# Where the attention outputs are turned, where the output projection's pieces stand, and a combination in two parts

## The chip, the cores and the metric

The kernel runs on one core of one Trainium2 chip. The metric is the device time of one execution in microseconds, of which the median of several executions is taken. The engines are called PE (TensorE, matrix multiply), ACT (ScalarE), DVE (VectorE), POOL (GpSimd) and SP (SyncE, which only issues transfers here).

## What is computed

Two layers of a transformer trunk on 1024 rows of 1024 columns, in float32. Cut to its core:

```python
for l in range(2):
    h = rmsnorm(x, g_mix[l])
    proj = h @ w_in[l]                       # q, k, v of 12 heads in three groups
    lam = exp(sum(l0 * l1)) - exp(sum(l2 * l3)) + lam_init
    # group A, 4 heads: a = softmax(s1) - lam * softmax(s2); o = rmsnorm(a @ v, g_sub) * (1 - lam_init)
    # group B, 4 heads: sliding window of 128 with sinks
    # group C, 4 heads: forgetting attention (a cumulated log gate is added to the scores)
    x = x + concat([o_a, o_b, o_c]) @ w_out[l]
    h = rmsnorm(x, g_mlp[l])
    x = x + square(relu(h @ w_up[l])) @ w_down[l]
return rmsnorm(x, g_final)
```

## The kernel before

Every large product is made in three passes, since each operand is split into a high and a low part of reduced precision: high by high, low by high, high by low. A **piece** is such a product of one 128x128 block of weights with one chunk of 128 rows of the activations (`accumulate`, L1134): six matmuls of 128x512. ACT makes the high parts (`w_hi`, `wide_hi`, `pt_hi`), DVE or POOL the low parts (`w_lo`, `wide_lo`, `pt_lo`).

In a layer, attention is done by 8 **pairs** of heads in turn (`ORDER`: B, B, C, C, A, A, A, A), each in 8 **steps**, one for each block of 128 query rows, so that step `t` runs from 0 to 63. Pair 6 is steps 48 to 55, and pair 7, the last, is steps 56 to 63. A step of pair A has, in this order of dependence: the scores on PE (`scores`, L1213; two phases when there are more than four key blocks), score plus bias with its row maximum on DVE (`biased_max`, L912), two exponentials on ACT (L638), the combination `a = p1 - lam * p2` on DVE (`combine`, L940), the transposes of the result on PE (`turn_half`, L1266; a **half** is up to four blocks of 128x128 and takes one of the two banks of `ps[2]`), high and low part of the transposed half (L656 on ACT, L963 on DVE), and the products with the values (`values`, L1286 and L1288). The sum of these goes to `o_out` (L972).

Work that does not depend on the step stands between. A step is cut into **slots**, one for each half that is turned in it; PE's order in a slot is scores, pieces, second phase of the scores, turn of the half, and the values of the half of the slot before. `PIECES` says how many pieces a step gets: in pairs 0 to 6 those of the in-projection slabs of the next pair (`FILL`), in pair 7 those of the output projection. An output slab `k` is 128 columns of `w_out`; its pieces go over the eight slabs of `o_out`. `OUT+k` is the number of its weights among the loads. In pair 7 the first three output slabs get six of their eight pieces each (O0, O1 and O2 below), the rest of them comes later from small copies of the weights (`xw_hi`, `xw_lo`). After step 63 comes a tail: output slab 3 in `ps[0]`, the last head's normalisation, and then the output slabs in the order `OFIN`.

Before a slab of `o_out` can be multiplied it is transposed into `wide_hi` and `wide_lo`: eight blocks, in two **mix halves** that use the same `ps[2]` banks, with L651 on ACT and L958 on DVE. `MIX_AT` says in which step each slab's mix halves stand, always at the step's end, in slots of their own. `SCALE_AT` says at which steps the A heads' norms are taken (variances on DVE, a square root on ACT with two table loads, the scaling on POOL). All engines run their programs in order, so that what stands behind a waiting instruction waits too; a turn of half `h` waits for the low part of half `h - 2`.

Of the kernel before, what the change touches and what calls it, by code (L numbers as in the profile page):

```python
# [44 lines left out]
def hybrid_encoder(nc, x, w_in, a_lambda, a_subln, b_sinks, c_fbias, w_out, g_mix, g_mlp,  # L45
# [44 lines left out]
    OFIN = [3, 0, 4, 1, 5, 2, 6, 7]  # L90
# [31 lines left out]
    NPHASE = PHASE0[NT]  # L122

# [3 lines left out]
    PIECES[PAIRS - 1] = [0, 1, 3, 4, 4, 3, 3, 0]  # L127
    MIX_AT = {56: [0, 1], 57: [2, 3], 58: [4, 5], 62: [6]}
    SCALE_AT = {FIRST_A * NQ + 2 * NQ + 3: (0, 2), FIRST_A * NQ + 3 * NQ + 3: (2, 3)}
# [83 lines left out]
    for t in range(NT):  # L213
        now = [s for s in slots if s.step == t]
        wide = phases(t) == 2
        for j in range(2):
            at = (j + 2 if len(now) >= 4 else j) if wide else 0
            now[min(at, len(now) - 1)].exps.append(j)
        now[1 if wide and len(now) >= 4 else 0].second = wide
# [11 lines left out]
    with ExitStack() as ctx:  # L231
# [302 lines left out]
        def _(act):  # L534
# [54 lines left out]
            for l in range(DEPTH):  # L589
# [69 lines left out]
                def finish_o(t):  # L659
# [3 lines left out]
                    if grp == "A":  # L663
                        A.activation(o_junk[:], o_out[:, p, i * P:(i + 1) * P], ACT.Square,
# [27 lines left out]
                if slots[-1].summed is not None:  # L692
                    finish_o(slots[-1].summed)
                finish_o(NT - 1)
                rms_of_heads(3, 4)
                split_load(l, EXTRA + 1)
# [65 lines left out]
        def _(dve):  # L762
# [48 lines left out]
            for l in range(DEPTH):  # L811
# [118 lines left out]
                def combine(t):  # L930
# [9 lines left out]
                    V.scalar_tensor_tensor(out=probs[:, (2 * t) % 4, 0:width], in0=probs[:, (2 * t + 1) % 4, 0:width],  # L940
                                           scalar=lam_ratio[:, c:c + 1], in1=probs[:, (2 * t) % 4, 0:width],
                                           op0=ALU.mult, op1=ALU.add).then_inc(combined, 1)
# [59 lines left out]
                for s in slots:  # L1002
# [3 lines left out]
                    if s.first and t < NT:  # L1006
                        biased_max(t, 0)
                    if s.first and t:
                        if ORDER[(t - 1) // NQ][0] == "A":
                            combine(t - 1)  # L1010
                        else:
                            invert_sums(t - 1)
                    if s.second:
# [18 lines left out]

                sum_values(NT - 1)
# [6 lines left out]
                split_load(l, EXTRA + 1)  # L1040
# [69 lines left out]
        def _(pe):  # L1110
# [40 lines left out]
            for l in range(DEPTH):  # L1151
# [95 lines left out]
                def turn_half(half):  # L1247
# [9 lines left out]
                    elif ORDER[half.step // NQ][0] == "A":  # L1257
                        pe.wait_ge(combined, NQ * AH * l + half.step - NQ * FIRST_A + 1)
# [33 lines left out]

                for s in slots:
# [10 lines left out]
                    dense(s.pieces[early:])  # L1304
                    if s.half:
# [4 lines left out]
                def out_piece(k, slab, p, start, stop):  # L1310
                    j = w_slot(l, OUT + k)
                    return accumulate(p, w_hi[:, j, chunk_of(slab)], w_lo[:, j, chunk_of(slab)], wide_hi[here][:, slab],
                                      wide_lo[here][:, slab], start, stop)

                pe.wait_ge(scores_read, NPHASE * (l + 1))
                pe.wait_ge(w_split, LOADS * l + OUT + 4)
                out_piece(3, 0, 0, True, False)
                out_piece(3, 1, 0, False, False)
                values(slots[-1].half)
                for slab in range(2, NC - 1):  # L1320
                    if slab == LATE:
                        pe.wait_ge(pt_split, NHALF * l + mix_ready[LATE])
                    out_piece(3, slab, 0, False, False)
                for half in MIX_LAST:
                    turn_half(half)
                for f, k in enumerate(OFIN):
                    p = FINAL_OUT_PS[f]
                    if f == 0:
                        pe.wait_ge(pt_split, NHALF * (l + 1))
                        out_piece(k, NC - 1, p, False, True).then_inc(slab_done, 1)  # L1330
                        continue
                    if f == 1:
                        pe.wait_ge(evacuated, EVACS * l + IN + NPARTIAL)
                        pe.wait_ge(w_split, LOADS * l + EXTRA + 1)
# [88 lines left out]
```

## Time and profile before

| | |
|---|---|
| median of 3 executions | 2730.36 us (2727.61 to 2734.29) |
| the profiled execution | 2732.85 us, of it 2730.8 us span |
| PE busy | 2586.2 us, 95% of the span |
| DVE, ACT, POOL busy | 42%, 33%, 8% |
| mean granted clock of PE | 0.98 of full |

The page lists busy times, the chain of work that ended last and groups of instructions; the trace behind it gives each instruction's start, and, for a wait, who ended it.

### The profile page before, as it was taken

What the parts mean: (1) busy time and instruction counts of PE and PEld (TensorE: products, weight loads), DVE (VectorE), ACT (ScalarE), POOL (GpSimd) and SP (SyncE); (2) the same over time, 40 slices, a digit from 0 to 9 for tenths busy, and PEclk for the clock granted to TensorE, in tenths of its full rate; (3) what the DMA queues carried; (4) which work ended last, traced back from release to release, by engine and by line L of the source; (5) the groups of instructions that cost most, each with busy time, mean ns of one, the idle gap of its engine ahead of it and who ended that gap; (6) DMA issues with size and microseconds to landing.
All of it is one profiled execution on the core that took longest, in us unless ns stands there. A gap on an engine that the chain in (4) does not pass through costs nothing.

```text
span 2730.8 us, 33929 instructions
## 1 busy us (share of the span) xinstructions
PE 2586.2 (95%) x12825; PEld 2117.3 (78%) x12825; DVE 1153.6 (42%) x2309; ACT 893.1 (33%) x1572; POOL 216.4 (8%) x101
## 2 busy tenths in 40 slices
PE   7999999879999999999999999987899999999998
PEld 6778777668788888888878777765788888888886
DVE  5555566645322223223336546665542232232233
ACT  4554444433211212112236544444322121120222
POOL 1111111112000000000211111111110000000001
PEclk9999999999999999999999999999999999999999
DMA  5100010211111111111220000002111111111112
GB/s 174 55 24 24 16 32 24 62 39 45 46 47 46 54 46 46 54 46 52 94 86 24 24 24 24 24 24 68 47 39 54 46 46 54 46 46 54 45 47 77
DMA packets 219019, 131.42 MB, mean 48 GB/s; under 512 B 15222, under 2 KB 214432, under 8 KB 218664
## 3 DMA queue, kind: packets, MB, share of 16 engines
q1 hardware_dynamic: 213208, 114.38, 14.5%
q10 hardware_dynamic: 5712, 15.73, 1.5%
q8 instruction: 61, 1.00, 0.2%
q14 instruction: 38, 0.31, 0.0%
HBM read 117.47 MB, written 12.62 MB: 48 GB/s over the span
## 4 chain that ended last, share of the span: by engine, by line
PE 75%; issue 9%; DVE 8%; ACT 6%; DVEq 2%; DMA 0%; SPq 0%; ACTq 0%; POOL 0%; POOLq 0%
PE ps L1134 67%; DVE probs L912 2%; PE ps L1266 2%; PE ps L1286 2%; ACT probs L638 2%; ACT pt_hi L656 2%; PE ps L1213 1%; PE ps L1288 1%; DVEq L919 1%; DVE pt_lo L963 1%; DVE probs L940 1%; DVE neg_max L927 1%; ACT sink_exp L641 1%; DVE part L823 0%; PE ps L1115 0%
## 5 line engine op out<-in xcount | busy, mean ns | idle before, releaser
L1134 PE MATMUL ps<-wide_hi,w_hi 128*128 128x512 f32 x3016 | 960.1, 400 | 41.2 <-DVE v_parts L833 10.6
L1134 PE MATMUL ps<-wide_lo,w_hi 128*128 128x512 f32 x3016 | 939.7, 393 | 0.0
L1134 PE MATMUL ps<-wide_hi,w_lo 128*128 128x512 f32 x3016 | 937.6, 392 | 0.0
L1134 PEld LDWEIGHTS ps<-wide_hi,w_hi 128*128 128x128 f32 x3016 | 553.7, 190 | 176.7 <-issue 54.9
L1134 PEld LDWEIGHTS ps<-wide_hi,w_lo 128*128 128x128 f32 x3016 | 571.8, 190 | 122.6
L1134 PEld LDWEIGHTS ps<-wide_lo,w_hi 128*128 128x128 f32 x3016 | 571.5, 190 | 122.5
L638 ACT ACTIVATE probs<-probs,neg_max,slope 128x256 f32<-128x256 f32 (+7 forms) x256 | 202.4, 791 | 339.1 <-DVE neg_max L927 275.3
L714 ACT ACTIVATE w_hi<-w_raw 128x1024 fp32r<-128x1024 f32 x112 | 117.8, 1052 | 453.0 <-PE ps L1134 443.5
L963 DVE TENSOR_TENSOR pt_lo<-ps,pt_hi 128x512 fp32r<-128x512 f32 (+3 forms) x216 | 126.6, 586 | 262.1 <-ACT pt_hi L656 261.7
L718 ACT ACTIVATE ring<-ring 128x1024 f32<-128x1024 f32 x64 | 67.8, 1060 | 491.0 <-DVE ring L1069 491.0
L1089 DVE TENSOR_TENSOR xt<-ps,xt 128x1024 f32 x48 | 58.8, 1225 | 387.1 <-PE ps L1134 387.1
L1069 DVE SCALAR_TENSOR_TENSOR ring<-ps,inv_rms 128x1024 f32<-128x1024 f32 x64 | 78.4, 1225 | 330.0 <-PE ps L1134 313.2
L1286 PE MATMUL ps<-v_parts,pt_hi 128*128 128x128 f32 (+1 forms) x696 | 187.2, 331 | 27.8 <-DVE pt_lo L963 27.6
L510 POOL TENSOR_TENSOR w_lo<-w_raw,w_hi 128x1024 fp32r<-128x1024 f32 x50 | 121.8, 2436 | 950.6 <-ACT w_hi L546 950.6
L1286 PEld LDWEIGHTS ps<-v_parts,pt_hi 128*128 128x128 f32 x696 | 137.0, 197 | 38.6 <-DVE pt_lo L963 37.0
L1288 PE MATMUL ps<-v_parts,pt_lo 128*128 128x64 f32 (+1 forms) x696 | 160.8, 240 | 0.0
L656 ACT ACTIVATE pt_hi<-ps 128x512 fp32r<-128x512 f32 (+3 forms) x216 | 109.0, 505 | 136.3 <-PE ps L1266 135.8
L1072 DVE TENSOR_TENSOR wide_lo<-ring,wide_hi 128x1024 f32 x64 | 78.4, 1226 | 158.1 <-ACT wide_hi L720 158.1
L1266 PE MATMUL ps<-ident,probs 128*128 128x128 f32 x696 | 117.7, 284 | 28.5 <-DVE probs L940 28.3
L1288 PEld LDWEIGHTS ps<-v_parts,pt_lo 128*128 128x128 f32 x696 | 138.0, 198 | 0.1
L1065 DVE TENSOR_TENSOR w_lo<-w_raw,w_hi 128x1024 fp32r<-128x1024 f32 x112 | 136.4, 1218 | 2.2 <-ACT w_hi L714 2.2
L1266 PEld LDWEIGHTS ps<-ident,probs 128*128 128x128 f32 x696 | 86.6, 145 | 57.6 <-issue 40.4
(139 smaller groups left out, 1836.5 us busy)
## 6 DMA issues: line engine op xcount, KB each, us to landing
w_raw<-in_w_up_dram SPq DMA_DIRECT2D x128, 256.0 KB, 3.0
w_raw<-in_w_down_dram SPq DMA_DIRECT2D x128, 256.0 KB, 3.0
w_raw<-in_w_in_dram SPq DMA_DIRECT2D x92, 256.0 KB, 3.3
x_saved<-xt ACTq DMA_DIRECT2D x16, 512.0 KB, 2.6
w_raw<-in_w_out_dram SPq DMA_DIRECT2D x32, 256.0 KB, 3.3
xt<-x_saved SPq DMA_DIRECT2D x16, 512.0 KB, 3.7
o_out<-cum_saved ACTq DMA_DIRECT2D x2, 2048.0 KB, 8.1
out_dram<-rows SPq DMA_DIRECT2D x4, 1024.0 KB, 5.7
```

What stands on the lines that cost most here:

```text
L510: nc.gpsimd.tensor_tensor(w_lo[:, j], w_raw[:], w_hi[:, j].bitcast(F32), ALU.subtract).then_inc(w_split, 1)
L638: e = A.activation(probs[:, (2 * t + j) % 4, 0:width], probs[:, (2 * t + j) % 4, 0:width], ACT.Exp, bias=neg_max[:, at:at + 1], scale=sl, ...
L656: A.activation(pt_hi[:, bank, 0:half.blocks], src.rearrange("p (b q) -> p b q", q=P), ACT.Copy).then_inc(pt_hi_done, 1)
L714: A.activation(w_hi[:, w_slot(l, FFN_DONE + j)], w_raw[:], ACT.Copy).then_inc(w_hi_done, 1)
L963: V.tensor_tensor(pt_lo[:, bank, 0:half.blocks], src.rearrange("p (b q) -> p b q", q=P), pt_hi[:, bank, 0:half.blocks].bitcast(F32), ALU.s ...
L1065: V.tensor_tensor(w_lo[:, z], w_raw[:], w_hi[:, z].bitcast(F32), ALU.subtract).then_inc(w_split, 1)
L1069: V.scalar_tensor_tensor(out=ring[j][:], in0=ps[j][:], scalar=0.0, in1=inv_rms[:], op0=ALU.max, op1=ALU.mult).then_inc(evacuated, 1)
L1072: V.tensor_tensor(u_lo[:, 2 * m + j], ring[j][:], u_hi[:, 2 * m + j].bitcast(F32), ALU.subtract).then_inc(u_split, 1)
L1134: mm = T.matmul(ps[p][:, bass.ts(t, BANK)], w, h[:, bass.ts(t, BANK)], start=(start and n == 0), stop=(stop and n == 2))
L1266: tr = T.transpose(ps[2][:, at:at + P], src[:, b * P:(b + 1) * P], ident[:])
L1286: T.matmul(o.rearrange("p (h e) -> p h e", h=2), pt_hi[:, bank, at], v_parts[:, kv_slot(p), k0 + b, :, e], start=(b == 0), stop=False)
L1288: mm = T.matmul(o[:, 0:w], pt_lo[:, bank, at], v_parts[:, kv_slot(p), k0 + b, 0, e], start=False, stop=(b == blocks - 1))
```

## The change

The tables change. The output slabs' first mix halves are turned from step 54 on, that is between the pieces of the last in-projection slab of pair 6. The 18 pieces of the output projection, which stood 0, 1, 3, 4, 4, 3, 3, 0 over the eight steps of pair 7 (what a slot can't hold moves on), stand 2, 2, 2, 2, 2, 2, 3, 3. The tail has slab 3's pieces spread between its halves, and puts seven of the eight pieces of output slab 4 into `ps[1]` before and after the last mix halves; `OFIN` has slab 4 second. Its weights are split earlier on ACT and DVE. `combine` is issued in two instructions where the row is over 512 wide, each with its own signal, and PE waits for the part it turns; at the first step of a pair A it stands ahead of `biased_max`. The second exponential no longer stands in a mix slot. One wait is added on ACT (`o_squared`).

```diff
-    OFIN = [3, 0, 4, 1, 5, 2, 6, 7]
+    OFIN = [3, 4, 0, 5, 1, 6, 2, 7]
...
-    PIECES[PAIRS - 1] = [0, 1, 3, 4, 4, 3, 3, 0]
-    MIX_AT = {56: [0, 1], 57: [2, 3], 58: [4, 5], 62: [6]}
-    SCALE_AT = {FIRST_A * NQ + 2 * NQ + 3: (0, 2), FIRST_A * NQ + 3 * NQ + 3: (2, 3)}
+    PIECES[PAIRS - 1] = [2, 2, 2, 2, 2, 2, 3, 3]
+    MIX_AT = {54: [0], 55: [1, 2], 56: [3, 4], 57: [5], 61: [6]}
+    SCALE_AT = {FIRST_A * NQ + 2 * NQ + 3: (0, 2), FIRST_A * NQ + 3 * NQ + 2: (2, 3)}
...
-        now = [s for s in slots if s.step == t]
+        now = [s for s in slots if s.step == t and (s.half is None or s.half.slab is None)]
...
+                        if NQ * (AH * l + n) + i:
+                            act.wait_ge(o_squared, NQ * (AH * l + n) + i)
...
+                split_load(l, EXTRA + 1)
                 finish_o(NT - 1)
                 rms_of_heads(3, 4)
-                split_load(l, EXTRA + 1)
...
-                    V.scalar_tensor_tensor(out=probs[:, (2 * t) % 4, 0:width], in0=probs[:, (2 * t + 1) % 4, 0:width],
-                                           scalar=lam_ratio[:, c:c + 1], in1=probs[:, (2 * t) % 4, 0:width],
-                                           op0=ALU.mult, op1=ALU.add).then_inc(combined, 1)
+                    for k0 in range(0, width, BANK):
+                        k1 = min(width, k0 + BANK)
+                        V.scalar_tensor_tensor(out=probs[:, (2 * t) % 4, k0:k1], in0=probs[:, (2 * t + 1) % 4, k0:k1],
+                                               scalar=lam_ratio[:, c:c + 1], in1=probs[:, (2 * t) % 4, k0:k1],
+                                               op0=ALU.mult, op1=ALU.add).then_inc(combined, 1)
...
-                    if s.first and t < NT:
+                    join = t % NQ == 0 and FIRST_A * NQ < t < NT
+                    if s.first and t < NT and not join:
                         biased_max(t, 0)
                     if s.first and t:
                         if ORDER[(t - 1) // NQ][0] == "A":
                             combine(t - 1)
                         else:
                             invert_sums(t - 1)
+                    if s.first and join:
+                        biased_max(t, 0)
...
+                    if t == NT:
+                        if s.first:
+                            pe.wait_ge(scores_read, NPHASE * (l + 1))
+                            pe.wait_ge(w_split, LOADS * l + OUT + 4)
+                        for slab in (0, 1) if s.first else (2, 3):
+                            out_piece(3, slab, 0, slab == 0, False)
...
-                out_piece(3, 0, 0, True, False)
-                out_piece(3, 1, 0, False, False)
+                out_piece(3, 4, 0, False, False)
                 values(slots[-1].half)
-                for slab in range(2, NC - 1):
-                    if slab == LATE:
-                        pe.wait_ge(pt_split, NHALF * l + mix_ready[LATE])
-                    out_piece(3, slab, 0, False, False)
+                out_piece(3, 5, 0, False, False)
+                pe.wait_ge(pt_split, NHALF * l + mix_ready[LATE])
+                out_piece(3, LATE, 0, False, False)
+                pe.wait_ge(evacuated, EVACS * l + IN + NPARTIAL)
+                pe.wait_ge(w_split, LOADS * l + EXTRA + 2)
+                for slab in range(5):
+                    out_piece(4, slab, 1, slab == 0, False)
                 for half in MIX_LAST:
                     turn_half(half)
+                for slab in range(5, NC - 1):
+                    out_piece(4, slab, 1, False, False)
+                pe.wait_ge(pt_split, NHALF * (l + 1))
+                out_piece(3, NC - 1, 0, False, True).then_inc(slab_done, 1)
+                out_piece(4, NC - 1, 1, False, True).then_inc(slab_done, 1)
```

**DVE, end of step 54 and start of step 55** of the first layer. Before: low parts of step 53's two halves, the sum of step 52's values, and then the first phase of step 55's maximum (L912).

```order
L963 TENSOR_TENSOR pt_lo_74<-ps2,pt_hi_73 128x512
L972 TENSOR_REDUCE o_out_88<-ps3 128x128
L963 TENSOR_TENSOR pt_lo_74<-ps2,pt_hi_73 128x256
L900 MEMSET wait_slot_118 128x1
L912 ISA probs1_67,row_max_108<-ps0,far_93 128x512
L912 ISA row_max_108 128x1
L912 ISA probs1_67,row_max_108<-ps0,far_93 128x512
```

Now, with its own line numbers (L966 is the low part of a mix half, L971 that of a half of step 53, L980 the sum of values, L918 the maximum):

```order
L971 TENSOR_TENSOR pt_lo_74<-ps2,pt_hi_73 128x512
L980 TENSOR_REDUCE o_out_88<-ps3 128x128
L971 TENSOR_TENSOR pt_lo_74<-ps2,pt_hi_73 128x256
L966 SCALAR_TENSOR_TENSOR wide_lo0_54<-ps2,mix_gain_97,wide_hi0_52 128x512
L980 TENSOR_REDUCE o_out_88<-ps3 128x128
L966 SCALAR_TENSOR_TENSOR wide_lo0_54<-ps2,mix_gain_97,wide_hi0_52 128x512
L906 MEMSET wait_slot_118 128x1
L918 ISA probs1_67,row_max_108<-ps0,far_93 128x512
```

Two low parts of mix halves and a sum of values have moved in between, ahead of the maximum for which PE's second phase of step 55 waits.

**DVE, end of step 55 and start of step 56.** Before: evacuation of the last in-projection slab (L826), low part, step 56's maximum, combination of step 55 (L940), low part of the values' operand (L833).

```order
L826 TENSOR_TENSOR part_82<-ps1,inv_rms_84 128x1024
L963 TENSOR_TENSOR pt_lo_74<-ps2,pt_hi_73 128x384
L900 MEMSET wait_slot_118 128x1
L912 ISA probs1_67,row_max_108<-ps0,far_93 128x128
L912 ISA row_max_108 128x1
L912 ISA probs1_67,row_max_108<-ps0,far_93 128x128
L912 ISA row_max_108 128x1
L927 TENSOR_SCALAR neg_max_110<-row_max_108,neg_slope_100 128x2
L935 RECIPROCAL inv_sum_113<-row_sum_111 128x1
L937 TENSOR_SCALAR lam_ratio_114<-inv_sum_113,a_sum_115,neg_lam_103 128x1
L940 SCALAR_TENSOR_TENSOR probs1_67<-probs1_67,lam_ratio_114 128x1024
L833 TENSOR_TENSOR v_parts1_65<-ps1,v_parts1_65 128x8x128
```

Now (L832 the evacuation, L948 the combination, L839 the values' operand):

```order
L966 SCALAR_TENSOR_TENSOR wide_lo0_54<-ps2,mix_gain_97,wide_hi0_52 128x512
L980 TENSOR_REDUCE o_out_88<-ps3 128x128
L832 TENSOR_TENSOR part_82<-ps1,inv_rms_84 128x1024
L966 SCALAR_TENSOR_TENSOR wide_lo0_54<-ps2,mix_gain_97,wide_hi0_52 128x512 x3
L941 RECIPROCAL inv_sum_113<-row_sum_111 128x1
L943 TENSOR_SCALAR lam_ratio_114<-inv_sum_113,a_sum_115,neg_lam_103 128x1
L948 SCALAR_TENSOR_TENSOR probs1_67<-probs1_67,lam_ratio_114 128x512 x2
L906 MEMSET wait_slot_118 128x1
```

The combination, in two parts of 512, has gone ahead of the maximum, and three more low parts of mix halves stand ahead of both; the maximum and then L839 follow.

**PE, from the end of step 55** into step 56. Now (L1145 is a piece's matmul, L1277 a turn, L1224 the scores, L1126 the transposes of the values' slab):

```order
L1145 MATMUL ps1<-wide_hi0_52,w_hi_50 128x512 x2
L1145 MATMUL ps1<-wide_lo0_54,w_hi_50 128x512 x2
L1145 MATMUL ps1<-wide_hi0_52,w_lo_51 128x512 x2
L1277 MATMUL ps2<-ident_90,o_out_88 128x128 x12
L1224 MATMUL ps0<-k_hi1_61,q_hi1_57 128x128 x2
L1224 MATMUL ps0<-k_lo1_63,q_hi1_57 128x128 x2
L1224 MATMUL ps0<-k_hi1_61,q_lo1_59 128x128 x2
L1126 MATMUL ps1<-ident_90,part_82 128x128 x8
L1277 MATMUL ps2<-ident_90,probs1_67 128x128 x4
L1145 MATMUL ps1<-wide_hi0_52,w_hi_50 128x512 x2
L1145 MATMUL ps1<-wide_lo0_54,w_hi_50 128x512 x2
```

Before, the scores of step 56 followed the values of step 54, and between the turn of step 55's first half and that of its second stood the values of step 54 and no piece:

```order
L1213 MATMUL ps0<-k_hi1_61,q_lo1_59 128x128 x2
L1115 MATMUL ps1<-ident_90,part_82 128x128 x8
L1266 MATMUL ps2<-ident_90,probs1_67 128x128 x4
L1286 MATMUL ps3<-v_parts1_65,pt_hi_73 128x256
L1288 MATMUL ps3<-v_parts1_65,pt_lo_74 128x128
```

A piece of the output projection stands behind the turn now, and three mix halves (x12) stand ahead of the scores.

## Rows read from the trace of the kernel before

**Rows 1.** Busy time in windows: stretch, busy of PE, PEld, DVE, ACT, POOL, clock, DMA share, GB/s.

```profile
640.00:1360.00 720.00, 717.80 (x3176) 594.35 (x3176) 214.79 (x176) 154.64 (x151) 23.56 (x10) 1.00 0.17 52
441.00:508.30 67.30, 61.02 (x318) 47.77 (x318) 40.55 (x112) 29.38 (x68) 11.51 (x5) 0.92 0.09 24
508.30:614.20 105.90, 81.47 (x441) 63.45 (x439) 57.37 (x149) 44.67 (x94) 11.39 (x5) 0.90 0.20 59
1843.00:1949.00 106.00, 80.43 (x443) 62.86 (x442) 57.54 (x149) 44.84 (x94) 11.40 (x5) 0.90 0.20 60
```

**Rows 2.** The same view by place: steps 54-58, 59-61, 62-63, tail of the first layer.

```profile
486.74:540.21 53.47, 42.90 (x242) 32.44 (x240) 31.12 (x82) 23.23 (x53) 4.78 (x2) 0.90 0.22 64
540.21:570.56 30.35, 25.59 (x132) 19.21 (x131) 15.61 (x49) 12.75 (x23) 5.61 (x3) 0.94 0.14 45
570.56:593.20 22.64, 15.23 (x87) 11.21 (x85) 14.37 (x39) 10.10 (x24) 3.40 (x2) 0.90 0.21 65
593.20:614.20 21.00, 17.43 (x88) 15.18 (x87) 8.00 (x13) 5.67 (x11) 0.00 (x0) 0.86 0.10 28
```

**Rows 3.** Who PE waited for, 508.3 to 620 us: total, times, longest.

```profile
PE ps L1266 <- DVE probs L940: 7.0, 5, 1.9
PE ps L1286 <- DVE pt_lo L963: 4.6, 5, 2.7
PE ps L1266 <- DVE wide_lo L958: 4.5, 4, 1.5
PE ps L1134 <- POOL w_lo L510: 3.3, 1, 3.3
PE ps L1213 <- DVE row_max L912: 3.2, 1, 3.2
PE ps L1134 <- DVE wide_lo L958: 1.8, 1, 1.8
```

**Rows 4.** PE in order of time, steps 54 to 57: start, length, what, [wait].

```profile
495.44 0.38 PE L1286 MATMUL ps<-v_parts,pt_hi 128*128 128x256 f32 x1 [1.60 <-DVE pt_lo L963]
...
507.28 0.38 PE L1286 MATMUL ps<-v_parts,pt_hi 128*128 128x256 f32 x1 [0.28 <-DVE pt_lo L963]
...
511.82 0.63 PE L1266 MATMUL ps<-ident,probs 128*128 128x128 f32 x4 [1.90 <-DVE probs L940]
...
531.25 1.05 PE L1134 MATMUL ps<-wide_lo,w_hi 128*128 128x512 f32 x2
```

**Rows 5.** DVE at the start of step 56, and a combination 512 wide.

```profile
510.39 1.28 DVE L940 SCALAR_TENSOR_TENSOR probs<-probs,lam_ratio 128x1024 f32<-128x1024 f32 x1
511.59 1.22 DVE L833 TENSOR_TENSOR v_parts<-ps,v_parts 128x1024 fp32r<-128x1024 f32 x1
...
548.39 0.75 DVE L940 SCALAR_TENSOR_TENSOR probs<-probs,lam_ratio 128x512 f32<-128x512 f32 x1
```

**Rows 6.** PE in order of time: a third mix half, and mix halves ahead of step 63.

```profile
539.62 0.66 PE L1266 MATMUL ps<-ident,o_out 128*128 128x128 f32 x4 [1.13 <-DVE wide_lo L958]
...
580.03 0.60 PE L1266 MATMUL ps<-ident,o_out 128*128 128x128 f32 x4
...
585.60 0.79 PE L1213 MATMUL ps<-k_hi,q_hi 64*128 64x512 f32 x2 [3.21 <-DVE row_max L912]
```

**Rows 7.** DVE in order of time ahead of step 63's maximum.

```profile
583.56 0.75 DVE L958 SCALAR_TENSOR_TENSOR wide_lo<-ps,mix_gain,wide_hi 128x512 fp32r<-128x512 f32 x1 [1.04 <-ACT wide_hi L651]
584.24 0.69 DVE L912 CUSTOM_DVE_ANT_0 probs<-ps,far 128x512 f32<-128x512 f32 x1
```

**Rows 8.** PE and DVE in order of time around output slab 3.

```profile
603.00 0.68 PE L1134 MATMUL ps<-wide_hi,w_hi 128*128 128x512 f32 x2
...
609.88 1.03 PE L1266 MATMUL ps<-ident,o_out 128*128 128x128 f32 x8
...
614.20 0.62 PE L1134 MATMUL ps<-wide_hi,xw_hi 128*128 128x512 f32 x2
...
619.76 1.21 DVE L791 TENSOR_TENSOR w_lo<-w_raw,w_hi 128x1024 fp32r<-128x1024 f32 x1
```

More of the change, by code:

```diff
@@ L122, in hybrid_encoder, with combined_at @@
     NPHASE = PHASE0[NT]
+    NCOMB = sum(phases(t) for t in range(FIRST_A * NQ, NT))
+    def combined_at(t, part):
+        return PHASE0[t] - PHASE0[FIRST_A * NQ] + part + 1
     PIECES = {0: [2] * 8, 1: [2] * 8, 2: [0, 3, 3, 3, 3, 4, 4, 4], 3: [3, 3, 3, 3, 3, 3, 3, 3]}
@@ L1031, in _ @@
                         invert_heads(*SCALE_AT[t - 1])
+                split_load(l, EXTRA + 1)
                 sum_values(NT - 1)
@@ L1039, in _ @@
                                 ALU.mult).then_inc(o_scaled, 1)
-                split_load(l, EXTRA + 1)
                 for half in MIX_LAST:
@@ L1257, in turn_half @@
                     elif ORDER[half.step // NQ][0] == "A":
-                        pe.wait_ge(combined, NQ * AH * l + half.step - NQ * FIRST_A + 1)
+                        pe.wait_ge(combined, NCOMB * l + combined_at(half.step, half.units[0][1] // 4))
                     at = BANK * bank
@@ L1291, in values, with out_piece @@
                     mm.then_inc(pt_used, 1)
+                def out_piece(k, slab, p, start, stop):
+                    j = w_slot(l, OUT + k)
+                    return accumulate(p, w_hi[:, j, chunk_of(slab)], w_lo[:, j, chunk_of(slab)], wide_hi[here][:, slab],
+                                      wide_lo[here][:, slab], start, stop)
                 for s in slots:
@@ L1308, in _ @@
                         values(s.values)
[L1310 to L1316, printed above, removed]
-                out_piece(3, 0, 0, True, False)
-                out_piece(3, 1, 0, False, False)
-                values(slots[-1].half)
-                for slab in range(2, NC - 1):
-                    if slab == LATE:
-                        pe.wait_ge(pt_split, NHALF * l + mix_ready[LATE])
-                    out_piece(3, slab, 0, False, False)
+                out_piece(3, 4, 0, False, False)
+                values(slots[-1].half)
+                out_piece(3, 5, 0, False, False)
[5 more added lines that the diff above has]
+                    out_piece(4, slab, 1, slab == 0, False)
                 for half in MIX_LAST:
                     turn_half(half)
+                for slab in range(5, NC - 1):
[3 more added lines that the diff above has]
+                out_piece(4, NC - 1, 1, False, True).then_inc(slab_done, 1)
                 for f, k in enumerate(OFIN):
+                    if f < 2:
+                        continue
                     p = FINAL_OUT_PS[f]
[L1328 to L1334, printed above, removed]
-                    elif f == 2:
+                    if f == 2:
                         pe.wait_ge(o_summed, NT * (l + 1))
```

## The prediction

> **What bounds the kernel now.** I read the windows first. Over 720 us of the first layer's MLP, PE is busy 717.8 us at clock 1.00 [rows 1]: nothing is to be had there. The stretch from step 56 to the first piece with the small weight copies is different: 105.90 us, PE busy 81.47, so 24.4 us idle, at a granted clock of 0.90; the second layer has the same, 80.43 of 106.00 [rows 1]. Pair 6 before it idles 67.30 - 61.02 = 6.3 us at 0.92. The change touches steps 54 to 63, the tail behind them, and in a small way every combination. It adds no matmul and removes none, so PE's idle time and clock in these stretches are all it can change, twice over (two layers).
>
> Then I cut the stretch by place [rows 2] and take PE's busy time from each: idle 53.47 - 42.90 = 10.6 us in steps 54 to 58, 4.8 in 59 to 61, 7.4 in 62 and 63, 3.6 in the tail; 26.3 us in all. The waits by releaser say whose fault it is [rows 3]: the combination 7.0, low parts of turned halves 4.6, low parts of mix halves 4.5 and 1.8, POOL's low part of a weight 3.3, a row maximum 3.2. Nearly all is DVE, though DVE is busy only 31.12 of 53.47 us in steps 54 to 58 [rows 2]: its queue is in order and each wait is the latency of a chain, not throughput.
>
> **The change, by place, one layer.** I walked the new order by hand with the durations of the old trace: a piece 1.38 us (five from 603.00 to 609.88 [rows 8]), the combination 1.28 for 1024, 0.75 for 512 [rows 5], and so on.
>
> *Steps 54 to 58.* Steps 54 and 55 now have one piece a slot, since the slab's pieces are spread over the mix slots too. PE waited 1.60 us in step 54 for the low part of a half, 0.28 in step 55 [rows 4]. Between scores and values one piece less stands in step 54 and two less in step 55, 4.1 us less cover; part of the chain gets shorter by the earlier combination, and I get 2.6 for each of the two steps: +3.3. Mix halves at the end of step 54 put two low parts and a sum ahead of step 55's maximum. The old trace has this pattern ahead of step 63: from the first mix turn at 580.03 to the released scores at 585.60 it takes 5.6 us, and PE waited 3.21 of it [rows 6]. DVE shows why: its mix low part waited 1.04 for ACT, and the maximum could start only behind it [rows 7]. In the new place PE has 3.6 us of its own work: +1.8. Step 55 has two slabs, so a third mix half needs a bank back: 1.13 us in the old trace [rows 6], the longest of its kind 1.5 [rows 3]; I take 1.4, as low parts of three queue: +1.4. At the start of step 56 the combination is put ahead of the maximum, but behind three mix low parts and the evacuation: about 1.25 us of them is in the way, and the values' operand L839 (1.22 us, 0.1 to 1.2 late [rows 5]) holds the first piece with it. I take 2.2 where 1.90 was [rows 4]: +0.3. In steps 56 to 58 the four old mix waits (4.45 of them [rows 3]) and the short ones in between (2.3) become 0.2 + 1.7, 1.2 and 1.8 for the halves and steps that replace them, and about 1.0 of short ones. Steps 54 to 58 thus go from 10.6 to about 2.6 + 2.6 + 1.8 + 1.4 + 2.2 + 5.9 = 16.5: **+6**. Bounds: +1, if step 54 and 55 stay at their old waits and the third halves cost 1.13; +9, if every mix half costs 1.5 and the maximum as much as 3.21.
>
> *Steps 59 to 61.* With two pieces a step, the first of a weight is asked for later than POOL delivers it: 3.3 goes. In its place stands step 61's mix pair ahead of step 62's maximum, 3.21 in the old place, less some for the pieces now beside it; I take 2.4, and 2.1 for the rest. 4.5 for 4.8: **-0.3**. Bounds -2.8, +1.
>
> *Steps 62 and 63.* The 3.21 ahead of step 63 goes, and six pieces, 8.3 us, stand in 62 and 63 where three stood; against that the last step's own chain (2.7 [rows 3]) is covered by 2.8 us of pieces in part. I get 5.3 for 7.4: **-2.0**. Bounds -5 (only the combination stays), 0.
>
> *The tail.* The two waits of 1.8 (combination, last mix low part) are covered: pieces of slab 3 stand before the turns, and slab 4's, 1.38 each, before and behind the last mix halves. Slab 4's weights are split early enough, since ACT and DVE idle there: busy 5.67 and 8.00 of 21.00 us [rows 2]. DVE's early split holds the last sum back by 1.2 us at most; the normalisation behind it has five pieces of slab 4 as cover, 6.9 us. But the third slab of the new order, output slab 0, needs only two small pieces, and then slab 5 wants weights whose low part DVE ends at 619.76 + 1.21 = 620.97, 6.8 us behind the end of slab 3 at 614.20 [rows 8]. PE gets there after three pieces, 4.1 us: a new wait of 2.7. It was covered by eight pieces of slab 4 before. 2.8 for 3.6: **-0.8**. Bounds -3.6 (DVE splits it sooner), +2.
>
> *Split combination.* The second half costs 2 x 0.75 - 1.28 = 0.2 us more on DVE [rows 5], and the turn of the first half starts 0.5 sooner. In pairs 4 to 6 the combination ends a short wait now and then: **-0.5** a layer, bounds +2, -2. The added wait on ACT is for a square taken a step before; it costs nothing, since DVE's variances and the whole step lie between.
>
> *My own error.* The durations with which I walked sum to about 96 us over the 127.4 us of rows 2, where PE's busy time sums to 101.2. So PE really gets to each wait later than in my walk; half of the 5 us falls ahead of a wait and shortens it: **-2.5**.
>
> *The clock.* It was granted 0.90, 0.94, 0.90 and 0.86 in the four places [rows 2], so 5.3, 1.8, 2.3 and 2.9 us were lost. A row shows the lower level: two matmuls of a piece take 1.05 us at 531.25 [rows 4], 0.62 at 614.20 [rows 8]. It fell behind waits: 1.5 at the mix halves before 531, 3.3 at POOL, 3.2 and 2.7 in step 63. Where these go I give the clock back: nothing in steps 54 to 58, where there is more waiting than before; 1.2 in 59 to 61; 1.1 in 62 and 63; all 2.9 in the tail: **-5.2**. Bounds 0 and -8.
>
> Sum: +6 - 0.3 - 2.0 - 0.8 - 0.5 - 2.5 - 5.2 = -5.3 us a layer, -10.6 for two. The profiled execution took 2732.85 us (2730.8 of it span), 2.5 above the median; the same change there gives 2722.2. From the median, 2730.36 - 10.6 = **2720**.
>
> The Trainium skill, page "VectorE: DVE Perf Modes", section "The TRN2 errata — SBUF-src ops pay a fixed extra latency per instruction", asks for tiles of at least 512 elements, because each instruction pays a fixed cost. The rows agree in kind: 0.75 for 512 is more than half of 1.28. By the page's formula of 58 cycles and one per element at 0.96 GHz, an estimate, the split would cost 0.06 us of DVE time, where the rows say 0.2. Its rule speaks against this split; rival C' below is what it would do here.
>
> **The rivals.**
>
> *A, likeliest, 0.45:* as summed, 8 to 20 us gained.
>
> *B, all of it spreads well, 0.20:* the last stretch becomes like pair 6, which has pieces in every slot and half the trouble. 81.47 x 67.30 / 61.02 = 89.9 us, and the clock 0.92 for 0.90 takes 1.8 off: 88.1 for 105.9, 17.8 a layer, 35.6 in all: 2695. For it: the mix halves no longer stand four in a row in steps without pieces. Against it: two pieces a step, not three.
>
> *C, moved, not removed, 0.17:* steps 54 to 58 lose what the rest gains. With the upper bound +9 there and the clock down there too (-3 instead of -5.2), 5.2 is lost of 5.3: about 2730. For it: each wait that I name there is a DVE queue in which mix low parts stand ahead of a maximum, seen at 585.60 [rows 6].
>
> *C', the split combination costs, 0.05:* one chain for two parts. 0.2 us for each of the wide combinations, five blocks or more, four a pair, 16 a layer, is 3.2, in place of the 0.5 gained: 3.7 a layer, 7.5 in all if all lies on PE's path: 2727. Against it: most combinations are not waited for.
>
> *D, slower, 0.13:* thin pieces and mix halves in steps 54 to 57 drop PE to half clock. The pattern of 580 to 592, a wait of 3.2 and the 1.7 us that it then lost at the lower level, would stand at three places (maximum of step 55, combination of 56, maximum of 58): 3 x 4.9 = 14.7 a layer, instead of the 6 in my sum, and the clock gain falls to 2: -5.3 + 8.7 + 3.2 = +6.6, +13 in all: 2744. It decides from +12 a layer in steps 54 to 58 on.
>
> **How the numbers follow.** 0.3% is 8.2 us, about what a measurement of this kernel can tell from no change. Faster than 2722.2: most of A (0.40 of 0.45) and B, 0.60. Within: the rest of A, C and C', 0.27. Slower than 2738.6: D, 0.13. The range leaves out the lower half of B and D: 2697 to 2735. A's own range is 2710 to 2722.
>
> **What the new profile would show.** Steps 54 and 55: PE's values wait for the low part L971 some 2.6 us each; PE's second phase of step 55 waits for the maximum L918 by 1.5 to 2; the first turn of step 56 waits for L948 by about 2; no wait on POOL's low part. Ahead of step 62 a wait for L918 of 2 to 3, none ahead of 63. In the tail no wait on L966, but one of 2 to 3 us on DVE's w_lo three pieces after slab 3 ends. Clock of the tail near 1.00. I am wrong if idle in steps 54 to 58 stays at 10 us (then B) or passes 20 (then D), if the clock in 59 to the tail does not rise above 0.94, or if the wait on w_lo is not there.

## The result, and the profile after

The changed kernel takes 2744.39 us in the median (2739.62 to 2745.84, five executions) where the one before took 2730.36: ratio 1.004, 95% interval 1.0026 to 1.0054. It is slower, and I had forecast 2720. The profiled execution, the fastest of the five, has a span of 2737.8 us, 7.0 more than before, with PE busy 2591.3 us (2586.2 before). Thus of the 7.0 us only 1.9 are idle time of PE (146.5 for 144.6), and 5.1 are matmuls that took longer.

The places of [rows 2] in the changed kernel, first layer and then second: steps 54 to 58, 59 to 61, 62 and 63, the tail to the first piece with the small weights (now with all eight pieces of slab 4 in it), and what follows. The columns are those of [rows 1].

```profile
489.83:549.48 59.65, 45.36 (x250) 34.71 (x248) 32.15 (x85) 23.28 (x51) 4.76 (x2) 0.91 0.23 71
549.48:573.96 24.48, 20.34 (x115) 15.37 (x114) 16.36 (x52) 13.43 (x30) 4.71 (x2) 0.93 0.08 22
573.96:597.74 23.78, 19.57 (x101) 14.46 (x101) 14.40 (x42) 9.22 (x19) 4.22 (x2) 0.93 0.20 62
597.74:622.56 24.82, 24.82 (x129) 21.04 (x128) 8.97 (x14) 5.71 (x11) 0.00 (x0) 1.00 0.15 43
622.56:645.00 22.44, 19.76 (x80) 15.87 (x79) 13.40 (x10) 11.02 (x11) 8.24 (x4) 0.92 0.16 47
1828.37:1890.38 62.01, 47.96 (x248) 36.80 (x246) 32.13 (x85) 23.65 (x52) 4.75 (x2) 0.86 0.22 68
1890.38:1915.59 25.21, 21.43 (x116) 16.48 (x115) 16.05 (x52) 13.48 (x30) 4.71 (x2) 0.86 0.07 21
1915.59:1939.50 23.91, 19.72 (x101) 14.57 (x101) 14.52 (x42) 9.20 (x19) 4.23 (x2) 0.93 0.20 61
1939.50:1964.21 24.71, 24.71 (x129) 20.86 (x128) 8.83 (x14) 5.71 (x11) 0.00 (x0) 1.00 0.15 43
```

Span less PE busy gives the idle time: 14.3, 4.1, 4.2 and 0.0 us in the first layer, and 14.1, 3.8, 4.2 and 0.0 in the second. The tail, at 0.86 before, now runs without a gap at 1.00.

PE in order of time, six of the waits that the prediction named:

```profile
497.73 0.38 PE L1297 MATMUL ps<-v_parts,pt_hi 128*128 128x256 f32 x1 [1.72 <-DVE pt_lo L971]
...
505.67 0.50 PE L1224 MATMUL ps<-k_hi,q_hi 64*128 64x512 f32 x2 [1.58 <-DVE row_max L918]
...
511.70 0.39 PE L1297 MATMUL ps<-v_parts,pt_hi 128*128 128x256 f32 x1 [2.35 <-DVE pt_lo L971]
...
524.20 0.63 PE L1277 MATMUL ps<-ident,probs 128*128 128x128 f32 x4 [1.66 <-DVE probs L948]
...
565.71 0.39 PE L1224 MATMUL ps<-k_hi,q_hi 64*128 64x256 f32 x2 [2.94 <-DVE row_max L918]
...
628.12 0.71 PE L1145 MATMUL ps<-wide_hi,w_hi 128*128 128x512 f32 x2 [2.68 <-DVE w_lo L797]
```

All six are there. I had 2.6, 1.8, 2.6, 2.2, 2.4 and 2.7 for them. No wait on L966 stands in the tail, and none on a maximum ahead of step 63, as forecast. So the part of the change that I looked at hardest did about what I said, and the loss is elsewhere: step 54 begins 3.1 us later than before already (489.83 for 486.74), where no table has changed anything. There, in pairs 4 to 6, only the combination differs (and the added wait on ACT, which the experiments below keep). PE around the start of step 48 and around step 53 in the changed kernel:

```profile
442.15 0.63 PE L1277 MATMUL ps<-ident,probs 128*128 128x128 f32 x4 [0.62 <-DVE probs L948]
...
444.70 0.80 PE L1145 MATMUL ps<-wide_hi,w_hi 128*128 128x512 f32 x2 [1.27 <-DVE v_parts L839]
...
446.15 1.05 PE L1145 MATMUL ps<-wide_hi,w_lo 128*128 128x512 f32 x2
...
485.73 0.85 PE L1145 MATMUL ps<-wide_hi,w_hi 128*128 128x512 f32 x2 [2.67 <-DVE part L832]
...
487.23 1.05 PE L1145 MATMUL ps<-wide_hi,w_lo 128*128 128x512 f32 x2
```

The wait on the combination has shrunk to 0.62, and 1.27 on the values' operand stands right behind it, for the 1.90 of before. At 485.73 PE waits 2.67 us for an evacuation (`part`; 1.41 before), and behind both the pieces run at the lower clock (1.05 for two matmuls). In the kernel before the clock is low behind these two waits as well, so these rows alone do not tell the loss:

```profile
441.62 0.73 PE L1266 MATMUL ps<-ident,probs 128*128 128x128 f32 x4 [1.90 <-DVE probs L940]
...
444.29 1.05 PE L1134 MATMUL ps<-wide_lo,w_hi 128*128 128x512 f32 x2
...
482.63 0.90 PE L1134 MATMUL ps<-wide_hi,w_hi 128*128 128x512 f32 x2 [1.41 <-DVE part L826]
483.33 1.06 PE L1134 MATMUL ps<-wide_lo,w_hi 128*128 128x512 f32 x2
```

What DVE did ahead of 485.73 in the changed kernel, by shapes (line, operation, shapes, count, busy us, mean ns, idle us before), and POOL in order of time:

```profile
L948 DVE SCALAR_TENSOR_TENSOR probs<-probs,lam_ratio 128x128 f32<-128x128 f32 x1 | 2.0, 1982 | 0.0
L948 DVE SCALAR_TENSOR_TENSOR probs<-probs,lam_ratio 128x512 f32<-128x512 f32 x1 | 0.8, 781 | 0.1
```

```profile
478.96 4.20 POOL L519 TENSOR_TENSOR o_out<-o_out,o_inv 128x1024 f32<-128x1024 f32 x2 [7.42 <-DVE o_inv L1002]
```

The second part of the combination is 128 wide and lasted 1982 ns: it stood until POOL's scaling was done at 483.16. The Trainium skill, page "SBUF — State Buffer", section "SBUF: two separate sides", says that a DVE instruction with both inputs in SBUF and a GpSimd instruction that reads SBUF exclude each other for a whole instruction; the row fits. In the kernel before, one instruction of 640 columns took 0.92 us beside the same scaling (DVE L940 at 478.67). That a combination in two parts has to ask for the port twice is my reading of this.

### The profile page after: what moved, and what is told of

Same layout as the page of the kernel before. It is cut to its first block, busy times and chain, and to the rows that moved or that the text cites. A ratio compares the mean times of both kernels' runs of the same rounds, so it can differ in the third digit from the quotient of the medians.

```text
span 2737.8 us, 34022 instructions
## 1 busy us (share of the span) xinstructions
PE 2591.3 (95%) x12825; PEld 2119.4 (77%) x12825; DVE 1159.5 (42%) x2341; ACT 893.6 (33%) x1572; POOL 215.7 (8%) x101
## 4 chain that ended last, share of the span: by engine, by line
PE 74%; DVE 8%; issue 8%; ACT 6%; DVEq 2%; DMA 0%; ACTq 0%; SPq 0%; POOL 0%; POOLq 0%
PE ps L1145 67%; DVE probs L918 2%; ACT probs L642 2%; PE ps L1297 2%; PE ps L1277 2%; ACT pt_hi L660 2%; PE ps L1224 1%; DVEq L925 1%; PE ps L1299 1%; ACT sink_exp L645 1%; DVE neg_max L933 1%; DVE pt_lo L971 1%; ACT wide_hi L655 1%; DVE probs L948 1%; DVE v_parts L839 0%
## 5 line engine op out<-in xcount | busy, mean ns | idle before, releaser
L1145 PE MATMUL ps<-wide_hi,w_hi 128*128 128x512 f32 x3016 | 965.9, 402 | 51.4 <-DVE v_parts L839 16.9
L1145 PE MATMUL ps<-wide_lo,w_hi 128*128 128x512 f32 x3016 | 943.4, 394 | 0.0
L1145 PE MATMUL ps<-wide_hi,w_lo 128*128 128x512 f32 x3016 | 941.5, 394 | 0.0
L1145 PEld LDWEIGHTS ps<-wide_hi,w_hi 128*128 128x128 f32 x3016 | 555.7, 191 | 188.4 <-issue 77.2
L1145 PEld LDWEIGHTS ps<-wide_lo,w_hi 128*128 128x128 f32 x3016 | 574.0, 190 | 123.4
L1145 PEld LDWEIGHTS ps<-wide_hi,w_lo 128*128 128x128 f32 x3016 | 574.0, 190 | 123.3
L971 DVE TENSOR_TENSOR pt_lo<-ps,pt_hi 128x512 fp32r<-128x512 f32 (+3 forms) x216 | 126.4, 586 | 274.7 <-ACT pt_hi L660 274.5
L1277 PE MATMUL ps<-ident,probs 128*128 128x128 f32 x696 | 115.1, 278 | 15.4 <-DVE probs L948 15.1
L1277 PEld LDWEIGHTS ps<-ident,probs 128*128 128x128 f32 x696 | 85.5, 142 | 45.0 <-issue 27.0
```

The costliest lines, as they stand in the source:

```text
L971: V.tensor_tensor(pt_lo[:, bank, 0:half.blocks], src.rearrange("p (b q) -> p b q", q=P), pt_hi[:, bank, 0:half.blocks].bitcast(F32), ALU.s ...
L1145: mm = T.matmul(ps[p][:, bass.ts(t, BANK)], w, h[:, bass.ts(t, BANK)], start=(start and n == 0), stop=(stop and n == 2))
L1277: tr = T.transpose(ps[2][:, at:at + P], src[:, b * P:(b + 1) * P], ident[:])
```

## The experiments

Ratios are to the kernel before, in the same job on the same chip, with 95% interval; "clock" is the mean of the granted clock over the executions. That of the kernel before is 0.981 (35 executions), of the changed one 0.977 (5).

**The combination in one instruction again,** all else as changed.

```diff
-                    for k0 in range(0, width, BANK): ... .then_inc(combined, 1)
+                    V.scalar_tensor_tensor(out=probs[:, (2 * t) % 4, 0:width], ...).then_inc(combined, phases(t))
```

> The changed kernel with the combination as one instruction again (one signal for both parts; everything else as changed). Ahead of step 54 PE idles 3.9 us more in the first layer and 2.6 us more in the second than before the change, and the tables move nothing there. Theory S, the split makes that idle time (it is one more instruction ahead of the evacuations, and at step 53 it stands beside POOL's scaling until 483.3): the 2.67 us wait on part at step 53 goes back to 1.41 us, and the kernel is 3 to 6 us faster than the changed one, ratio to before 1.002. Rival J, it comes from the combination standing ahead of the maximum at the start of a pair: the waits on v_parts of 1.27 stay, and the time stays within 2 us of the changed kernel, ratio 1.004.

Ratio 0.9979 (0.9966 to 0.9993), clock 0.983, 2727.11 us in the median. The same stretch of PE as above:

```profile
441.98 0.63 PE L1275 MATMUL ps<-ident,probs 128*128 128x128 f32 x4 [1.15 <-DVE probs L946]
443.86 0.70 PE L1143 MATMUL ps<-wide_hi,w_hi 128*128 128x512 f32 x2 [0.61 <-DVE v_parts L839]
...
482.18 0.71 PE L1143 MATMUL ps<-wide_hi,w_hi 128*128 128x512 f32 x2 [1.41 <-DVE part L832]
```

S in kind, and three times its size: 17 us for 3 to 6. The wait is back at 1.41, and the pieces behind both waits run at full clock (0.70, 0.71). Over the profiled executions, 12.1 us apart, PE's idle time fell from 146.5 to 143.5 us and its busy time by 9.1: three quarters of the difference are the same matmuls, which took longer.

All of it arises in steps 32 to 53 (pairs 4 to 6 up to the first moved mix half), where both kernels have the same 920 matmuls (a count can take in one or two at the edges). The windows, first and second layer, of the changed kernel and then of this run:

```profile
308.43:489.83 181.40, 163.18 (x921) 128.82 (x920) 117.30 (x332) 80.52 (x187) 23.34 (x10) 0.97 0.09 24
1647.45:1828.37 180.92, 162.97 (x920) 128.82 (x920) 117.28 (x332) 80.24 (x187) 23.30 (x10) 0.97 0.09 24
309.45:484.74 175.29, 160.20 (x922) 127.10 (x921) 114.70 (x322) 78.93 (x184) 23.46 (x10) 0.99 0.09 25
1641.47:1815.99 174.52, 158.55 (x920) 125.44 (x920) 114.47 (x322) 79.03 (x184) 23.48 (x10) 1.00 0.10 25
```

That is 12.5 us for the two layers, of it 5.1 idle (36.2 for 31.1) and 7.4 busy. So the split adds idle time here, and elsewhere 2.1 us of it are made good. Who PE waited for in this stretch of the first layer (total, times, longest) says where; the changed kernel, then this run:

```profile
PE ps L1145 <- DVE part L832: 4.7, 3, 2.7
PE ps L1145 <- DVE v_parts L839: 4.4, 3, 1.9
PE ps L1277 <- DVE probs L948: 3.1, 5, 0.8
```

```profile
PE ps L1275 <- DVE probs L946: 5.1, 7, 1.2
PE ps L1143 <- DVE part L832: 2.9, 3, 1.4
PE ps L1143 <- DVE v_parts L839: 1.8, 3, 0.6
```

The split ends 2.0 us of waits on the combination, and the waits on what DVE does next, the evacuation and the values' operand, grow by 4.4.

**The old tables,** with new tail and split combination (the three lines of PIECES, MIX_AT and SCALE_AT put back).

> The changed kernel with the old tables for pieces, mix halves and scaling; the new tail, order of output slabs and split combination stay. Theory M (the moved mix halves and thin steps cost what they give): PE's idle time in steps 54 to 58 goes from 14.3 back to some 10.6 us, POOL's wait of 3.3 and step 63's of 3.2 come back, and the time stays within 4 us of the changed kernel, ratio 1.003 to 1.005. Rival D (the tables are the loss): it goes back to before's time or under, ratio 0.998 to 1.000, some 11 us or more off the changed kernel.

1.0037 (1.0024 to 1.0050), clock 0.978: M. The waits on POOL (3.31) and ahead of step 63 (3.21) are back, and the time is not. The tables are not the loss.

**The new tables alone,** in the kernel before.

> The kernel before with the new tables alone: old tail, old order of output slabs, one combination, behind the maximum. Theory M: the steps 54 to 58 lose 2 to 4 us of idle time a layer, steps 59 to 63 gain 3 to 4; ratio to before 0.999 to 1.001. Rival D: 1.003 or more, with the granted clock of steps 54 to 61 near 0.86.

1.0008 (0.9999 to 1.0017), clock 0.981: M again, no change that can be told.

**Another order of the output slabs,** to cover the wait on slab 5's weights.

```diff
-    OFIN = [3, 4, 0, 5, 1, 6, 2, 7]
+    OFIN = [3, 4, 0, 1, 2, 5, 6, 7]
```

> The changed kernel with the output slabs finished in the order 3, 4, 0, 1, 2, 5, 6, 7, so that three slabs of two small pieces each stand ahead of slab 5, whose weights were waited for. Theory W: the wait of 2.68 us on DVE's low part w_lo behind the end of slab 0 goes, and nothing comes in its place: 5 us faster than the changed kernel in all, ratio 1.002. Rival V: the wait moves, to the evacuation of a bank or to slab 6's weights, since three slabs end within 8 us and DVE takes 1.2 us for each and 2 us for its low part: time as the changed kernel, 1.004.

1.0038 (1.0024 to 1.0052): V. PE in its tail waits for two evacuations (1.00 and 3.88) where 2.68 were:

```profile
628.03 0.73 PE L1145 MATMUL ps<-wide_hi,xw_hi 128*128 128x512 f32 x2 [1.00 <-DVE xt L1064]
...
634.94 1.22 PE L1145 MATMUL ps<-wide_hi,w_hi 128*128 128x512 f32 x2 [3.88 <-DVE xt L1064]
```

**The split combination alone,** in the kernel before (the loop, its count of signals and PE's wait).

> The kernel before with the split combination alone (two instructions, two signals, PE waits for its part). Theory S (the split is what makes the change slower, by itself): slower than before by 6 to 15 us, ratio 1.002 to 1.005, PE's idle time at most 3 us more and the rest a mean granted clock under 0.979. Rival X (the split costs only together with the moved mix halves or the combination ahead of the maximum): within 4 us of before, 0.999 to 1.001.

1.0020 (1.0005 to 1.0036), clock 0.978. S, at its lower edge, with an interval that reaches X, and PE's idle time over the profiled execution is that of the kernel before (144.6). The twelve executions fall into two groups, four at 2729 to 2733 us with a clock of 0.980 to 0.982 and eight at 2741 to 2744 with 0.976 to 0.978. Of 35 of the kernel before, five are above 2738. The split makes the lower clock frequent, not certain, and it costs less in the kernel before (0.2%) than in the changed one (0.6%).

**One combination, behind the maximum** (`join = False`).

> The changed kernel with one combination, and it stands behind the maximum at the start of a pair, as before the change. New tables and new tail stay. Theory N (the place at the start of a pair is worth nothing, since the values' operand releases the next piece): as the run with one combination, ratio 0.997 to 0.999. Rival J (with one combination the early place is what makes it faster than before): 3 us or more slower than that, 0.9995 or above.

0.9985 (0.9971 to 0.9998): N, though the interval reaches J. The early place at a pair's start is worth nothing that can be told from 0.9979.

**One combination, old tables.**

> The changed kernel with one combination and the old tables: new tail, new order of output slabs and the place ahead of the maximum stay. Theory T (tables give nothing, as the run of the tables alone and the run with old tables and split combination say): ratio 0.997 to 0.999, as with the new tables. Rival U (the tables give their 2 to 5 us a layer once DVE has no second combination ahead of the low parts): 1.000 or above.

0.9991 (0.9980 to 1.0002): between T and U, the interval touches both. Against 0.9979 the tables are worth some 0.1% with the new tail, which the intervals don't tell from nothing.

**Two instructions, both signals with the second.**

```diff
-                                               op0=ALU.mult, op1=ALU.add).then_inc(combined, 1)
+                                               op0=ALU.mult, op1=ALU.add)
+                    e.then_inc(combined, phases(t))
```

> The changed kernel, whose combination is in two instructions, but both signals come with the second, so PE's first turn isn't released early. It tells DVE's added time from the early release. Theory S1 (the second instruction's own time delays what stands behind it): as the changed kernel, ratio 1.003 to 1.006. Rival S2 (the early release spreads PE's waits over more places, and that costs clock): as with one combination, 0.998 to 1.000.

1.0008 (0.9998 to 1.0018), clock 0.982. Neither wins: it lies halfway. Over the whole execution PE is idle for 147.2 us (143.5 with one combination, 146.5 in the changed kernel), at a mean clock near that of one combination. Yet steps 32 to 53, first and second layer, are as slow as in the changed kernel:

```profile
306.91:488.64 181.73, 164.37 (x922) 129.97 (x921) 117.25 (x332) 80.36 (x187) 23.27 (x10) 0.96 0.09 24
1644.04:1826.73 182.69, 164.83 (x920) 130.06 (x920) 117.30 (x332) 80.29 (x187) 23.30 (x10) 0.96 0.09 24
```

So the second instruction is enough for the loss there, with no early release. What the late signals save lies behind it, in this one trace above all in steps 54 to the tail of the second layer, with a clock of 0.95 for 0.90.

**Slab 5's weights split before slab 3's parts,** with one combination.

```diff
+                    if c == 3:
+                        split_load(l, OUT + c + 3)
                     prepare(2 * l, f, c, h_hi, 2 * NC * l + NC + c)
-                    if c in (3, 4, 5):
+                    if c in (4, 5):
```

and the same around `h_low` on DVE.

> The changed kernel with one combination, and slab 5's weights are split before the high and low part of slab 3's normalised columns, on ACT and on DVE. Theory W (the wait of 2.7 us a layer on w_lo is a matter of DVE's order): it goes, and the kernel is 4 to 6 us faster than the one with one combination alone, ratio 0.995 to 0.997. Rival V (as with the reordered slabs, the wait moves to an evacuation): within 2 us of it, 0.998.

0.9943 (0.9930 to 0.9956): W, and a little more: 0.36% less than with one combination alone. No wait on `w_lo` stands in the two tails, and nothing in its place. PE's idle time is 138.5 us for 143.5.

**The first scaling one step later,** in the changed kernel with its split (`SCALE_AT` has `2 * NQ + 4` for `2 * NQ + 3`).

> The changed kernel, split combination and all, with POOL's first scaling of the heads one step later, so that it no longer runs beside the combination of step 52 and the evacuation for step 53. Theory P (a good part of the split's price is this meeting with POOL): the wait of 2.67 us on part goes to about 1.5 in both layers, the lower clock behind it too, and the kernel is 4 us or more faster than the changed one, ratio 1.0025 or less. Rival Q (POOL stalls another DVE instruction instead, or the clock falls elsewhere): 1.003 to 1.005.

1.0030 (1.0015 to 1.0044), clock 0.978. P's mechanism holds for the waits: PE is idle for 29.0 us in steps 32 to 53 (36.2 in the changed kernel). The two parts take 1.01 us together, and PE's wait is 1.04 for 2.67, but the piece behind it still falls to the lower clock. DVE, then PE:

```profile
480.16 1.01 DVE L948 SCALAR_TENSOR_TENSOR probs<-probs,lam_ratio 128x512 f32<-128x512 f32 x2
```

```profile
483.59 1.15 PE L1145 MATMUL ps<-wide_hi,w_hi 128*128 128x512 f32 x2 [1.04 <-DVE part L832]
```

The time is at Q's lower end, and its interval takes in P's 1.0025 and the changed kernel's 1.0040: the meeting with POOL makes the longest wait of the split, and what it is worth in time can't be told.

**All three: one combination, slab 5 early, scaling later.**

> The changed kernel with one combination, slab 5's weights split early, and the first scaling one step later: the best version that the runs so far point to. If W and P both hold, 0.994 to 0.996; if only W holds, as the run with the early split.

0.9939 (0.9927 to 0.9952), 2715.17 us: better than both kernels, 16.5 us under the one before in its job. From 0.9943, without the later scaling, it can't be told.

**The new tail alone with slab 5 early** (old tables, `join = False`).

> The new tail alone: the old tables, one combination behind the maximum as before the change, with slab 5's weights split early. Theory W with tables worth nothing: 0.996 to 0.998. If the tables are worth their part with this tail, 0.998 to 0.999, worse than with them.

0.9991 (0.9982 to 0.9999). W is wrong here: the early weights gain nothing over 0.9991 without them. So the new tables together with the early place of the combination, which no run parts here, are worth 0.5% once the tail has no wait, and some 0.1% while it has one. The clock is 0.979 here and 0.985 with the new tables.

**The split in the last pair only, and in pairs 4 to 6 only.**

```diff
+                    part = BANK if t >= (PAIRS - 1) * NQ else 2 * BANK
-                    for k0 in range(0, width, BANK):
+                    for k0 in range(0, width, part):
```

The second run has `t <` for `t >=`; in both the count of signals follows `part`.

> The changed kernel, with the combination in two parts only in the last pair (steps 56 to 63), one part in pairs 4 to 6. Theory E (the split does its harm in pairs 4 to 6, where the old and the changed trace differ ahead of step 54): as with one combination everywhere, 0.997 to 0.999. Rival L (in the last pair): 1.002 or more.

> The reverse: two parts in pairs 4 to 6 alone. Theory E: as the changed kernel, 1.003 to 1.005. Rival L: 0.997 to 1.000.

0.9980 (0.9969 to 0.9992) in the last pair, 1.0045 (1.0030 to 1.0059) in pairs 4 to 6. This is E. The windows of steps 32 to 53, first and second layer, first of the kernel before:

```profile
308.31:486.74 178.43, 163.08 (x921) 129.63 (x921) 115.38 (x323) 80.47 (x187) 23.45 (x10) 0.97 0.09 24
1647.02:1823.11 176.09, 159.80 (x922) 126.65 (x921) 114.55 (x322) 79.03 (x183) 23.45 (x10) 0.99 0.09 25
```

With the split in the last pair only:

```profile
306.43:481.36 174.93, 158.63 (x922) 125.42 (x921) 114.64 (x322) 79.03 (x184) 23.49 (x10) 1.00 0.09 25
1640.77:1815.29 174.52, 158.46 (x922) 125.41 (x921) 114.51 (x322) 79.05 (x184) 23.45 (x10) 1.00 0.09 25
```

With the split in pairs 4 to 6 only:

```profile
307.56:488.08 180.52, 162.19 (x922) 128.08 (x921) 117.36 (x332) 80.88 (x187) 23.52 (x11) 0.97 0.09 24
1645.12:1827.81 182.69, 164.36 (x922) 129.84 (x921) 117.36 (x332) 80.46 (x187) 23.28 (x10) 0.96 0.09 24
```

The split costs 13.8 us in this stretch of the two layers, 4.3 of it idle (36.7 for 32.4) and 9.5 in the same matmuls, with the clock at 0.97 and 0.96 for 1.00. The profiled executions of all runs agree on the idle part: with the split and POOL's scaling where the changed kernel has it, PE is idle for 35.2 to 36.7 us in steps 32 to 53 (six kernels), with one combination for 31.1 to 33.0 (eight). The clock is less clean: the kernel before, with one combination, also shows 0.97 in the first layer.

**The best version with the split put back.**

> The best version so far (one combination, slab 5's weights early, scaling one step later) with the split combination put back. If the split costs by itself in any arrangement, 8 us or more slower than the best version: ratio to before 0.997 or above. If it only cost by its meeting with POOL and by the order of this tail, 0.994 to 0.996.

0.9989 (0.9979 to 1.0000), against 0.9939: the split costs 0.5%, 14 us, in this arrangement too, where POOL isn't in its way. Steps 32 to 53 take 172.82 and 172.52 us in the best version at a clock of 1.00, and 176.95 and 178.24 with the split at 0.98 and 0.97; the idle time grows there by only 1.7 us, 28.6 to 30.3.

## Why the prediction was wrong

*The bound, and steps 54 to the tail: right.* Idle time by place was forecast as 16.5, 4.5, 5.3 and 2.8 us, before the correction for my own durations; it is 14.3, 4.1, 4.2 and 2.7, together 25.3 for 26.3 in [rows 2]. My sum less the 2.5 was 26.7. The six waits shown were where I put them, within 0.9 us. The wait on slab 5's weights, worked out from [rows 8] as 2.7, is 2.68, and with the new tables it was worth more than its own time: without it the kernel is 0.36% faster (0.9943 for 0.9979).

*The split combination: the step that failed.* I put -0.5 us a layer on it, with +2 and -2 as bounds, and rival C' at +3.7 a layer with a chance of 0.05. It measured +17 us for two layers in the changed kernel (1.0040 with it, 0.9979 without), by taking it out. Halving it by pairs (1.0045 and 0.9980) and adding it to the best version (14 us) agree; put into the kernel before by itself, it costs 0.2%, some 5 us. I costed it as DVE time and as the wait that it ends, and took the balance for a gain. The wait on the combination did get shorter, but the ones behind it grew by more: idle time in steps 32 to 53 rose by 3.1 us in the first layer and 2.0 in the second. And the same matmuls took 3.0 and 4.4 us longer, at a clock of 0.97 for 0.99 and 1.00. My bounds had no term for that, since I had charged the clock only to the stretch of the moved tables.

*The clock: the second.* I gave back 5.2 us a layer, nothing in steps 54 to 58, the rest behind them. The lost time by rows is now 5.4, 1.7, 1.7 and 0.0, and 1.8 behind the new wait on weights, 10.6 together for 12.3 before in the first layer. In the second it is 8.7, 3.5, 1.7 and 0.0. The tail gave its 2.9 back as forecast, 59 to 63 some 0.7 of their 2.3, and the new wait took 1.8 away. Of my three signs of being wrong the one on the clock shows in the second layer: it is 0.95 from step 59 to the end of the tail in the first layer and 0.93 in the second, where I asked for more than 0.94. Without the split the change gives 0.2%, some 6 us, where my sum without its term for the split was 9.6.

*The rivals.* D's 2744 is the measured time, and that is luck: steps 54 to 58 cost 3.7 us of idle time in the first layer, far from its +12, and the tables alone make no difference (1.0008). C', the split, had the right part of the change and less than half its price; its 3.2 us a layer, all idle time, are near the idle part (3.1 and 2.0 in steps 32 to 53), and it had no clock either. The Trainium skill's rule to have tiles of at least 512 elements (page "VectorE: DVE Perf Modes", section "The TRN2 errata — SBUF-src ops pay a fixed extra latency per instruction") speaks against the parts of 128, 256 and 384 that rows of 640, 768 and 896 leave. A fixed cost for each instruction is seen even with two parts of 512, in the row below, DVE in order of time in the changed kernel: 1.41 us for 1.28 in one instruction [rows 5]. It is 0.13 where I had 0.2, and over 32 wide combinations in two layers that is some 4 us of DVE time, an estimate, which can be a part of the 17 and not the whole.

```profile
376.25 1.41 DVE L948 SCALAR_TENSOR_TENSOR probs<-probs,lam_ratio 128x512 f32<-128x512 f32 x2
```

*Open.* Why the granted clock falls more often with the split isn't settled. The idle time in steps 32 to 53 is not equal: it is 4 to 5 us higher with the split. But in the best version 1.7 us more already came with 0.98 and 0.97 instead of 1.00. Over whole executions late signals have a mean clock of 0.982 and early ones 0.977, while the steps in which the split does its harm show 0.96 with late signals too. So the early release can at most have a part in what happens behind them; I can't say from these traces by what rule. The clock of a stretch is that of one profiled execution for each kernel.

## What to carry over

A kernel whose PE is 95% busy can lose more to the granted clock than to idle time: compare span times clock as well as waits. Here that product, with the means of all executions, is 2678 us for the kernel before and for the changed one, so that by this measure the whole difference is the clock; it counts a low clock during PE's waits too, and in the two profiled executions 5.1 of 7.0 us are slower matmuls. Compare idle time over the same instructions, not over the same microseconds: a window fixed in time holds fewer matmuls in the slower kernel, and so hides idle time that an edit adds. An edit that ends a wait earlier only to have the next wait behind it (0.62 and 1.27 for 1.90) gives nothing, and should be run by itself first, above all when it is applied everywhere and the rest of the change in one place. And a wait that is predicted should be mended before the first run: splitting one weight earlier gave 0.36%, some 10 us for waits of 5.4, with the new tables; with the old ones it gave nothing (0.9991 with and without).

## What was not expected of the hardware

A DVE instruction of 128 elements beside a scaling on POOL took 1982 ns, until POOL was done, where the 512 elements ahead of it took 781. The times of one kernel (the split alone) fall into two groups some 11 us apart, with clocks of 0.981 and 0.977, and how often each is seen was shifted by the split, which left PE's idle time over the whole execution at 144.6 us.
